# Scan of a hybrid layer: the doubling steps of two groups of token tiles are issued together over the four quarters of the array

## The chip, the cores and the metric

One core of one Trainium2 chip runs the program. The time is that of the device for one execution, in microseconds; the median of three runs is given. The records are of one further, profiled execution.

## What is computed

One layer of a backbone: a mixer of two branches (a 2-D Fourier transform, and a bidirectional RWKV-7 scan over 16 heads of 64 channels), normalised, then a feed-forward part with 16 experts. The change lies in the scan alone:

```python
def wkv7_scan(r, w, k, v, kk, a, s0, reverse):
    def step(S, inp):
        r_t, w_t, k_t, v_t, kk_t, a_t = inp
        sa = jnp.einsum('bhij,bhj->bhi', S, -kk_t)
        S = (S * w_t[:, :, None, :] + sa[..., None] * (kk_t * a_t)[:, :, None, :]
             + v_t[..., None] * k_t[:, :, None, :])
        y = jnp.einsum('bhij,bhj->bhi', S, r_t)
        return S, y
```

## The kernel before, in words

`scan_phase` computes the recurrence in blocks of 128 tokens: four of the latent sequence, one of the context. It walks over eight **tiles** of 128 channels, two heads each (`tiles`, `body`). In a tile, for each token block (`p`, in the order ORDER), direction and head, a unit triangular matrix of 128 x 128 has to be inverted; these are 5 x 4 problems. Each falls into two diagonal quarters of 64 x 64, which stand in partitions 0 to 63 and 64 to 127 and are inverted by doubling, and one quarter off the diagonal.

A tile has these stages:

1. *Pair products* (`pair_products`, L883 to L898): per token block the products of keys and queries, which DVE masks (L1192), and the quarters in both orientations, which ACT evicts to TT_diag and M (L772, L773; M is named `x` in the records, as it lies in spare room of that name). All four quarters of the PE array are used there: rows and columns 0 to 63 and 64 to 127 in every combination. POOL makes the start values: TT_diag (`tt_start`, L653 and L655), the masked blocks Mo of a level (`m_off`, L672) and T (`t_start`, L660, L664). Between the blocks stand pieces of the previous tile's norm.
2. *Doubling*, levels 1 to 5 (a round each, `rd` = 0 to 4), over three groups of token blocks: group 0 has two, group 1 two, group 2 one. In a round each group does Z = Mo by TT_diag (`z_step`, L914), ACT evicts Z (L781), then the increments of TT (L939) and of T (L945) in `t_step`, and DVE adds them (L1235, in the fifth round L1238 into TT; L1241). Group b's next Z needs its TT, its next TT increment needs its T. A group's matmuls alternate between two quarters of the array: rows 0 to 63 into output partitions 0 to 63, and rows 64 to 127 into 64 to 127. `m_off` overwrites the only buffer Mo, and so waits until the Z of the level before has been issued.
3. *Last level* (`rd` = 5): Z (L920), the product with T (L935), evicted by ACT into TT (L793).
4. *Chain* (L973 on): the states over the token blocks and the output.

Into the rounds are woven 14 **slots** that prepare the next tile, three per round, on every engine in the same order (`front`): slot 0 is a product of 512 columns (L830), its sigmoids on ACT (L701, after a table load) and a square (L706); slot 1 the same for 128 columns, after which DVE runs five prefix scans (L1092); then the norm of keys, the rates, exponentials (L739), operands (L1119 to L1124), all on DVE. Slot 0 on PE waits until ACT has read what stood in the bank before, slot 1 until slot 0's sigmoids are done. Two pieces of the previous tile's norm lie on DVE in slots 2 (L1179) and 14 (L1183, the gate product). The last tile has no slots; a few fillers (L951) keep PE going. The order on each engine is written out by hand, and an engine does its list strictly in order. A wait on PE holds everything behind it.

What sets the order around the change on PE in round 1 (lines 1026 on):

```python
                for rd in range(TOP):
                    z_step(i, NGR * rd)
                    z_step(i, NGR * rd + 1)
...
                    for b in range(NGR):
                        if b == 1:
                            z_step(i, NGR * rd + 2)
                        if not last and PER_ROUND * rd + b < NSLOT:
                            front(PER_ROUND * rd + b, i + 1, 1 - m)
...
                        t_step(i, NGR * rd + b)
```

## Time and profile before

| | us |
|---|---|
| median of 3 runs (2639.53 to 2642.63) | 2639.89 |
| the profiled execution | 2641.52 |
| its span, first to last instruction | 2639.6 |
| PE busy (matmuls) | 2402.4 (91%) |
| DVE busy | 1012.1 (38%) |
| ACT busy | 639.0 (24%) |
| POOL busy | 364.8 (14%) |
| L914 busy, L939 busy (3200 records each) | 116.6, 120.2 |

The span holds the projection, the scan (from 493 to about 1307 us), the merge and the experts. Busy time is the union of an engine's records. A matmul in f32 stands as two records in the profile, each as long as its passage through the array; records that overlap count once. The engine's idle time before an instruction stands in brackets with what released it; an idle engine costs something only where the end waits for it. PEclk is the share of TensorE's full clock that was granted. The shares of the whole span say little on the scan, since its stages have different limits; the windows below take its stages one by one.

### The profile page before, as it was taken

How to read it: one execution, taken by the hardware profiler on the slowest of the kernel's cores; microseconds unless marked ns; L12 is line 12 of the kernel's file. 1: busy time of each engine (PE TensorE's matmuls, PEld its weight loads, DVE VectorE, ACT ScalarE, POOL GpSimd, SP SyncE). 2: the span in 40 equal slices, each digit the busy share in tenths (PEclk: the TensorE clock that was granted, in tenths of full speed). 3: DMA queues.
4: the chain of work that ended last, by engine and by line, in shares of the span. 5: the costliest groups of instructions: out<-in, count | busy, mean ns of one | idle time of the engine just before them, and what ended most of it. 6: DMA issues, size and time to landing. Idle time of an engine off the chain costs nothing. (4 is left out here: it accounts for less than half of the span.)

```text
span 2639.6 us, 58406 instructions
## 1 busy us (share of the span) xinstructions
PE 2402.4 (91%) x26357; PEld 1534.5 (58%) x26357; DVE 1012.1 (38%) x1765; ACT 639.0 (24%) x1209; POOL 364.8 (14%) x405
## 2 busy tenths in 40 slices
PE   6999996689998999989799669999999999999993
PEld 4999995587787777778695423333333333333331
DVE  3343311658467576574345511212121212121214
ACT  2121222435445345343320101111111111111111
POOL 0000000315325225134003400000000000000000
PEclk7999998799999999999999779999999999999997
DMA  9362331010000000000191199999999999999974
GB/s 352 133 220 95 114 114 61 20 44 5 27 25 5 27 26 5 27 8 5 46 315 63 55 396 385 404 384 404 382 404 385 404 385 403 384 404 382 404 295 164
DMA packets 181119, 538.62 MB, mean 204 GB/s; under 512 B 13398, under 2 KB 54070, under 8 KB 180744
## 3 DMA queue, kind: packets, MB, share of 16 engines
q1 hardware_dynamic: 177704, 524.34, 52.3%
q0 software_dynamic: 3072, 10.49, 1.9%
q8 instruction: 209, 3.42, 0.5%
q14 instruction: 38, 0.31, 0.0%
q10 hardware_dynamic: 96, 0.05, 0.0%
HBM read 504.15 MB, written 30.70 MB: 203 GB/s over the span
## 5 line engine op out<-in xcount | busy, mean ns | idle before, releaser
L1815 PE MATMUL ps_h_lat<-w_piece,xT 128*64 128x512 f32 x2048 | 457.0, 599 | 10.9 <-DVE hidden L1937 7.5
L1815 PEld LDWEIGHTS ps_h_lat<-w_piece,xT 128*64 128x64 f32 x2048 | 145.9, 138 | 315.3 <-issue 315.3
L1840 PE MATMUL ps_y_lat<-w_piece,hiddenT 128*64 128x512 f32 x1024 | 232.6, 596 | 0.9 <-ACT hiddenT L1701 0.9
L1931 DVE TENSOR_TENSOR hidden<-sigmoid_lat,ps_h_lat 64x1024 f32<-64x1024 f32 x32 | 39.1, 1223 | 506.5 <-ACT sigmoid_ctx L1707 506.5
L1824 PE MATMUL ps_h_ctx<-w_piece,xT 128*16 128x512 f32 x2048 | 226.1, 593 | 0.0
L325 PE MATMUL ps_in<-hT_hi,w_in_hi 128*128 128x320 f32 x752 | 173.7, 312 | 2.7 <-issue 2.7
L672 POOL TENSOR_TENSOR Mo<-x,levels_sb 128x256 f32<-128x256 f32 x200 | 161.8, 832 | 99.0 <-PE ps_scan L914 98.9
L325 PE MATMUL ps_in<-hT_hi,w_in_lo 128*128 128x320 f32 x752 | 172.0, 310 | 0.0
L325 PE MATMUL ps_in<-hT_lo,w_in_hi 128*128 128x320 f32 x752 | 171.9, 310 | 0.0
L914 PE MATMUL ps_scan<-TT_diag,Mo 64*64 64x64 f32 x3200 | 116.6, 221 | 43.7 <-issue 26.9
L1840 PEld LDWEIGHTS ps_y_lat<-w_piece,hiddenT 128*64 128x64 f32 x1024 | 70.2, 137 | 138.3 <-issue 137.7
L1705 ACT ACTIVATE sigmoid_lat<-ps_h_lat 64x1024 f32<-64x1024 f32 x32 | 32.6, 1019 | 470.0 <-PE ps_h_lat L1815 470.0
L1824 PEld LDWEIGHTS ps_h_ctx<-w_piece,xT 128*16 128x16 f32 x2048 | 58.9, 97 | 139.9 <-issue 137.7
L914 PEld LDWEIGHTS ps_scan<-TT_diag,Mo 64*64 64x64 f32 x3200 | 106.3, 136 | 50.8 <-issue 49.3
L325 PEld LDWEIGHTS ps_in<-hT_hi,w_in_hi 128*128 128x128 f32 x752 | 126.2, 189 | 4.9 <-issue 4.7
L325 PEld LDWEIGHTS ps_in<-hT_lo,w_in_hi 128*128 128x128 f32 x752 | 126.5, 189 | 0.0
L325 PEld LDWEIGHTS ps_in<-hT_hi,w_in_lo 128*128 128x128 f32 x752 | 126.1, 189 | 0.0
L939 PE MATMUL ps_scan<-Z,T 64*64 64x64 f32 x3200 | 120.2, 222 | 5.6 <-ACT Z L781 5.3
L1756 POOL DMA_INDIRECT x_scratch<-ye,row_out x16 | 22.8, 1428 | 737.5 <-DVE ye L1944 737.5
L939 PEld LDWEIGHTS ps_scan<-Z,T 64*64 64x64 f32 x3200 | 107.2, 137 | 22.4 <-issue 19.0
L1192 DVE TENSOR_TENSOR NRR<-ps_scan,causal_sb 128x384 f32<-128x384 f32 x160 | 78.0, 549 | 104.7 <-PE ps_scan L884 104.6
L1849 PE MATMUL ps_y_ctx<-w_piece,hiddenT 128*16 128x256 f32 x2048 | 116.7, 380 | 0.0
(301 smaller groups left out, 3645.1 us busy)
## 6 DMA issues: line engine op xcount, KB each, us to landing
w_piece<-in_w_e SPq DMA_DIRECT2D x192, 2048.0 KB, 17.2
...
```

Of the source, the lines that this page charges most:

```text
L325: last = pe.matmul(wide[c % 2][:, b * 512:b * 512 + HALF], w, h[:, k, b * HALF:(b + 1) * HALF], start=(k == 0 and n == 0), stop=(k == KD - ...
L672: ins = g_.tensor_tensor(Mo[:, p, :, :].rearrange("p (e h) n -> p e h n", e=2), Mq[:, ORDER[p], 0:2, :, :], levels[:, l, :, :].unsqueeze(2 ...
L914: last = pe.matmul(ps_of(b_z(b), b)[hs, c, q, :], Mo[hs, p, q, :], TD[hs, p, q, :], start=True, stop=True)
L939: last = pe.matmul(ps_of(b_z(b), b)[hs, c, q, :], T[hs, p, q, :], Z[hs, p, q, :], start=True, stop=True)
L1192: v.tensor_tensor(NRR[:, p, :, :], src[:, 0:3 * P].rearrange("p (a n) -> p a n", a=3), causal[:, dr, :, :], ALU.mult).then_inc(s_am, 1)
L1705: act.activation(sg[UP, :], psA[UP, :], ACT.Sigmoid)
L1756: g_.indirect_dma_start(out=d["x1"], out_offset=bass.IndirectOffsetOnAxis(ap=row[j][:, 0:1], axis=0), in_=ye[j][:, :], in_offset=None, com ...
L1815: last = pe.matmul(psA[rows, cs], x[:, k, A], w[:, q, cs], start=(k == 0), stop=(k == KD - 1))
L1824: last = pe.matmul(psB[GRP[g], :], x[:, k, B], w[:, q, c * 512:(c + 1) * 512], start=(k == 0), stop=(k == KD - 1))
L1840: last = pe.matmul(psY[rows, :], hT[:, f, A], w[:, q, c * 512:(c + 1) * 512], start=(hf == 0 and f == 0), stop=(hf == 1 and f == FK - 1))
L1849: last = pe.matmul(psYB[GRP[g], 0:256], hT[:, f, B], w[:, q, g * 256:(g + 1) * 256], start=(hf == 0 and f == 0), stop=(hf == 1 and f == FK ...
L1931: v.tensor_tensor(hid[A, :], sg[UP, :], psA[UP, :], ALU.mult)
```

## The change

Token blocks 2 and 3 in the order (group 1) are CROSSED: their Z comes out in the other half of the partitions, and their T is held there too. So the matmuls of group 1 use the two quarters that group 0 leaves free, and `z_step` and `tt_step` take both groups together and alternate between them, four quarters in turn. The products that update T (`dt_step`) stay in two quarters each and stand by themselves; group 2's is issued after the next round's Z of both groups. For the crossed blocks the pair products compute T's start once more in the swapped place (8 matmuls a block), ACT evicts it (2 a block), and `t_start` masks it in place. Mo has two buffers, by the level's parity, and `m_off` waits for the Z of two levels before. The two pairs of fillers in the last level go. The orders on PE, ACT and DVE are written anew.

```diff
@@ -449,6 +449,7 @@
     NG, NPROB = NT, 4
     ORDER = [0, 3, 1, 2, 4]
     POS = {g: n for n, g in enumerate(ORDER)}
+    CROSSED = (2, 3)
     GROUPS, CHUNKS, BANKS = ((0, 2), (2, 4), (4, 5)), (slice(0, 4, 3), slice(1, 3, 1), slice(4, 5, 1)), ((0, 1), (2, 3), (4, 5))
     TOP = LEVELS - 1
     steps = [(b, l) for l in range(1, LEVELS) for b in range(len(GROUPS))]
@@ -495,7 +496,8 @@
 
         TT, M = [spare[:, n * NG * NPROB * P:(n + 1) * NG * NPROB * P].rearrange("p (g q n) -> p g q n", g=NG, q=NPROB)
                  for n in range(2)]
-        T, Z, Mo, TD = [sb(n, [P, NG, NPROB, HD]) for n in ("T", "Z", "Mo", "TT_diag")]
+        T, Z, TD = [sb(n, [P, NG, NPROB, HD]) for n in ("T", "Z", "TT_diag")]
+        Mo = [sb(f"Mo{n}", [P, NG, NPROB, HD]) for n in range(2)]
 
         y, gT = sb("y_T", [P, TOK])[:, :], sb("output_gate", [P, TOK])
         Mq = M.rearrange("p g q n -> p g (q n)")[:, :, 0:3 * 2 * HD].rearrange("p g (e h n) -> p g e h n", e=3, h=2)
@@ -657,7 +659,8 @@
                 def t_start(b):
 
                     for p in range(*GROUPS[b]):
-                        g_.tensor_tensor(T[:, p, :, :].rearrange("p (e h) n -> p e h n", e=2), Mq[:, ORDER[p], 0:2, :, :],
+                        low = T[:, p, :, :].rearrange("p (e h) n -> p e h n", e=2)
+                        g_.tensor_tensor(low, low if p in CROSSED else Mq[:, ORDER[p], 0:2, :, :],
                                          levels[:, 0, :, :].unsqueeze(2).broadcast_to([P, 2, 2, HD]), ALU.mult)
                     g_.drain()
                     flat = wide_of(T, b).rearrange("p c q n -> p (c q) n")
@@ -666,10 +669,10 @@
                 def m_off(n):
 
                     b, l = steps[n]
-                    if l > 1:
-                        g_.wait_ge(s_z, i * NS + n - NGR + 1)
+                    if l > 2:
+                        g_.wait_ge(s_z, i * NS + n - 2 * NGR + 1)
                     for p in range(*GROUPS[b]):
-                        ins = g_.tensor_tensor(Mo[:, p, :, :].rearrange("p (e h) n -> p e h n", e=2), Mq[:, ORDER[p], 0:2, :, :],
+                        ins = g_.tensor_tensor(Mo[l % 2][:, p, :, :].rearrange("p (e h) n -> p e h n", e=2), Mq[:, ORDER[p], 0:2, :, :],
                                                levels[:, l, :, :].unsqueeze(2).broadcast_to([P, 2, 2, HD]), ALU.mult)
                     ins.then_inc(s_mo, 1)
 
@@ -769,6 +772,8 @@
                 for n, g in enumerate(ORDER):
                     act.wait_ge(s_m, i * NG + n + 1)
                     for h in range(2):
+                        if n in CROSSED:
+                            act.activation(T[:, n, h::2, :], b_m(h)[:, 5 * HD:7 * HD].rearrange("p (e n) -> p e n", e=2), ACT.Copy)
                         act.activation(TD[:, n, h::2, :], b_m(h)[:, 3 * HD:5 * HD].rearrange("p (e n) -> p e n", e=2), ACT.Copy)
                         ins = act.activation(Mq[:, g, :, h, :], b_m(h)[:, 0:3 * HD].rearrange("p (e n) -> p e n", e=3), ACT.Copy)
                     ins.then_inc(s_ms, 1)
@@ -780,11 +785,9 @@
                         act.wait_ge(s_z, i * NS + NGR * rd + b + 1)
                         act.activation(wide_of(Z, b)[:, :, 0:nq, :], ps_of(b_z(b), b, nq), ACT.Copy).then_inc(s_zs, 1)
 
-                    evict(0)
-                    evict(1)
                     for b in range(NGR):
-                        if b == 1:
-                            evict(2)
+                        evict(b)
+                    for b in range(NGR):
                         if not last and PER_ROUND * rd + b < NSLOT:
                             front(PER_ROUND * rd + b, i + 1, 1 - m)
                         if rd == TOP - 1:
@@ -896,54 +899,60 @@
                     for x, xs in enumerate(HALVES):
                         for h, hs in enumerate(HALVES):
                             last = pe.matmul(b_m(h)[xs, (3 + dr) * HD:(4 + dr) * HD], B[dr][hs, at(x)], AR[m][dr][hs, g, 0, xs], start=True, stop=True)
+                    if n in CROSSED:
+                        for x, xs in enumerate(HALVES):
+                            for h, hs in enumerate(HALVES):
+                                last = pe.matmul(b_m(h)[HALVES[1 - x], (5 + dr) * HD:(6 + dr) * HD], AR[m][dr][hs, g, 0, xs], B[dr][hs, at(x)],
+                                                 start=True, stop=True)
                 last.then_inc(s_m, 1)
 
-            def z_step(i, n):
-                b, l = steps[n]
+            def problems(bs, l):
+
+                both = [[(b, c, p, q, x) for c, p in enumerate(range(*GROUPS[b])) for q in range(2 if l == TOP else NPROB) for x in range(2)]
+                        for b in bs]
+                return [one for pair in zip(*both) for one in pair]
+
+            def z_step(i, rd, bs):
+                l, n = rd + 1, NGR * rd + bs[-1]
                 if l < TOP:
                     pe.wait_ge(s_mo, i * ND + n + 1)
                 if l == 1:
-                    pe.wait_ge(s_tt0, i * NG + GROUPS[b][1])
+                    pe.wait_ge(s_tt0, i * NG + GROUPS[bs[-1]][1])
                 else:
                     pe.wait_ge(s_tt, i * ND + n - NGR + 1)
                 pe.sem_inc(s_pe_turn, 1)
...
+                for b, c, p, q, x in problems(bs, l):
                     if l < TOP:
-                        for q in range(NPROB):
-                            for hs in HALVES:
-                                last = pe.matmul(ps_of(b_z(b), b)[hs, c, q, :], Mo[hs, p, q, :], TD[hs, p, q, :], start=True, stop=True)
+                        last = pe.matmul(ps_of(b_z(b), b)[HALVES[x ^ (p in CROSSED)], c, q, :], Mo[l % 2][HALVES[x], p, q, :], TD[HALVES[x], p, q, :],
+                                         start=True, stop=True)
                     else:
-                        g = ORDER[p]
-                        for h in range(2):
-                            for dr, hs in enumerate(HALVES):
-                                os_ = HALVES[1 - dr]
-                                last = pe.matmul(ps_of(b_z(b), b, 2)[hs, c, h, :], Mq[os_, g, 2, h, :], TT[os_, g, 2 * dr + h, os_], start=True, stop=True)
-                last.then_inc(s_z, 1)
-
-            def t_step(i, n):
-                b, l = steps[n]
+                        g, os_ = ORDER[p], HALVES[1 - x]
+                        last = pe.matmul(ps_of(b_z(b), b, 2)[HALVES[x ^ (p in CROSSED)], c, q, :], Mq[os_, g, 2, q, :], TT[os_, g, 2 * x + q, os_],
+                                         start=True, stop=True)
+                last.then_inc(s_z, len(bs))
+
+            def tt_step(i, rd, bs):
+                l, n = rd + 1, NGR * rd + bs[-1]
                 pe.wait_ge(s_zs, i * NS + n + 1)
                 if l == 1:
-                    pe.wait_ge(s_ti, i * NGR + b + 1)
+                    pe.wait_ge(s_ti, i * NGR + bs[-1] + 1)
                 else:
                     pe.wait_ge(s_t, i * ND + n - NGR + 1)
                 pe.sem_inc(s_pe_turn, 1)
+                for b, c, p, q, x in problems(bs, l):
+                    hs, ts = HALVES[x], HALVES[x ^ (p in CROSSED)]
+                    if l == TOP:
+                        last = pe.matmul(ps_of(b_z(b), b, 2)[hs, c, q, :], T[ts, p, 2 * x + q, :], Z[ts, p, q, :], start=True, stop=True)
+                    else:
+                        last = pe.matmul(ps_of(b_z(b), b)[hs, c, q, :], T[ts, p, q, :], Z[ts, p, q, :], start=True, stop=True)
+                last.then_inc(s_dtt, len(bs))
+
+            def dt_step(b):
                 for c, p in enumerate(range(*GROUPS[b])):
-                    if l == TOP:
-                        for h in range(2):
-                            for dr, hs in enumerate(HALVES):
-                                last = pe.matmul(ps_of(b_z(b), b, 2)[hs, c, h, :], T[hs, p, 2 * dr + h, :], Z[hs, p, h, :], start=True, stop=True)
-                    else:
-                        for q in range(NPROB):
-                            for hs in HALVES:
-                                last = pe.matmul(ps_of(b_z(b), b)[hs, c, q, :], T[hs, p, q, :], Z[hs, p, q, :], start=True, stop=True)
-                last.then_inc(s_dtt, 1)
-                if l < TOP:
-                    for c, p in enumerate(range(*GROUPS[b])):
-                        for q in range(NPROB):
-                            for hs in HALVES:
-                                last = pe.matmul(ps_of(b_dt(b), b)[hs, c, q, :], Z[hs, p, q, :], T[hs, p, q, :], start=True, stop=True)
-                    last.then_inc(s_dt, 1)
+                    for q in range(NPROB):
+                        for hs in HALVES:
+                            last = pe.matmul(ps_of(b_dt(b), b)[hs, c, q, :], Z[hs, p, q, :], T[hs, p, q, :], start=True, stop=True)
+                last.then_inc(s_dt, 1)
 
             def fill(n):
 
@@ -1012,19 +1021,30 @@
                 pe.wait_ge(s_ms, i * NG + NG)
                 if not first:
                     pe.wait_ge(s_gs, i)
+                def slot(n):
+                    if not last and n < NSLOT:
+                        front(n, i + 1, 1 - m)
+
                 for rd in range(TOP):
-                    z_step(i, NGR * rd)
-                    z_step(i, NGR * rd + 1)
+                    z_step(i, rd, (0, 1))
+                    if rd:
+                        dt_step(2)
+                    z_step(i, rd, (2,))
                     if rd == TOP - 1:
                         turn(J_KT0, i, m, last)
-                    for b in range(NGR):
-                        if b == 1:
-                            z_step(i, NGR * rd + 2)
-                        if not last and PER_ROUND * rd + b < NSLOT:
-                            front(PER_ROUND * rd + b, i + 1, 1 - m)
-                        if rd == TOP - 1 and b:
-                            fill(2)
-                        t_step(i, NGR * rd + b)
+                        slot(PER_ROUND * rd)
+                        tt_step(i, rd, (0, 1))
+                        slot(PER_ROUND * rd + 1)
+                        tt_step(i, rd, (2,))
+                        slot(PER_ROUND * rd + 2)
+                    else:
+                        slot(PER_ROUND * rd)
+                        tt_step(i, rd, (0, 1))
+                        dt_step(0)
+                        slot(PER_ROUND * rd + 1)
+                        dt_step(1)
+                        tt_step(i, rd, (2,))
+                        slot(PER_ROUND * rd + 2)
                 fill(3)
                 pe.wait_ge(s_full, i * NGR + NGR)
                 part(i, m, CT, "X")
@@ -1222,23 +1242,38 @@
                         norm(n, i - 1, 1 - m)
                 for dr in range(2):
                     scaled_state(m, dr, 0)
+                def slot(n):
+                    if not first and n in (2, NSLOT):
+                        norm(N_BONUS if n == 2 else N_GATE, i - 1, 1 - m)
+                    if not last and n < NSLOT:
+                        front(n, i + 1, 1 - m)
+
+                def add_tt(rd, b):
+                    v.wait_ge(s_dtt, i * NS + NGR * rd + b + 1)
+                    if rd < TOP - 2:
+                        v.tensor_tensor(wide_of(TD, b), wide_of(TD, b), ps_of(b_z(b), b), ALU.add).then_inc(s_tt, 1)
+                    else:
+                        for hs in HALVES:
+                            ins = v.tensor_tensor(TT[hs, CHUNKS[b], :, hs], wide_of(TD, b)[hs], ps_of(b_z(b), b)[hs], ALU.add)
+                        ins.then_inc(s_tt, 1)
+
+                def add_t(rd, b):
+                    v.wait_ge(s_dt, i * ND + NGR * rd + b + 1)
+                    v.tensor_tensor(wide_of(T, b), wide_of(T, b), ps_of(b_dt(b), b), ALU.add).then_inc(s_t, 1)
+
                 for rd in range(TOP):
...
+                    if rd:
+                        add_t(rd - 1, 2)
+                    slot(PER_ROUND * rd)
+                    if rd < TOP - 1:
+                        add_tt(rd, 0)
+                        add_tt(rd, 1)
+                        add_t(rd, 0)
+                    slot(PER_ROUND * rd + 1)
+                    if rd < TOP - 1:
+                        add_t(rd, 1)
+                        add_tt(rd, 2)
+                    slot(PER_ROUND * rd + 2)
                 for n in CHAIN[:-1]:
                     state(i, m, n)
 
```

On **PE**, the first round of a middle tile; L914 is Z in the kernel before, L926 in the changed one, L939 or L947 TT's increment, L945 or L954 T's, L830 or L833 slots 0 and 1. Before:

```order
L914 MATMUL ps_scan<-TT_diag,Mo 64x64 x32
L830 MATMUL ps_scan<-lora,w_dec 128x512 x2
L939 MATMUL ps_scan<-Z,T 64x64 x16
L945 MATMUL ps_scan<-T,Z 64x64 x16
L914 MATMUL ps_scan<-TT_diag,Mo 64x64 x8
L830 MATMUL ps_scan<-lora,w_dec 128x128 x2
L939 MATMUL ps_scan<-Z,T 64x64 x16
L945 MATMUL ps_scan<-T,Z 64x64 x16
```

Changed:

```order
L926 MATMUL ps_scan<-TT_diag,Mo 64x64 x40
L833 MATMUL ps_scan<-lora,w_dec 128x512 x2
L947 MATMUL ps_scan<-Z,T 64x64 x32
L954 MATMUL ps_scan<-T,Z 64x64 x16
L833 MATMUL ps_scan<-lora,w_dec 128x128 x2
L954 MATMUL ps_scan<-T,Z 64x64 x16
L947 MATMUL ps_scan<-Z,T 64x64 x8
```

The 40 are Z of groups 0 and 1 (32) and of group 2 (8): group 2's Z now stands ahead of slot 0 and of the first TT increment.

On **DVE**, the same round from slot 0's end on; L1235 or L1254 is the add of TT, L1241 or L1262 that of T, L1092 or L1112 the prefix scans of slot 1. Before:

```order
L1235 TENSOR_TENSOR TT_diag<-TT_diag,ps_scan 128x512
L1241 TENSOR_TENSOR T<-T,ps_scan 128x512
L1092 SCALAR_TENSOR_TENSOR G_T<-one_sb,sg 128x128 x5
L1094 TENSOR_SCALAR half_total<-G_T 128x5
L1235 TENSOR_TENSOR TT_diag<-TT_diag,ps_scan 128x512
L1241 TENSOR_TENSOR T<-T,ps_scan 128x512
```

Changed:

```order
L1254 TENSOR_TENSOR TT_diag<-TT_diag,ps_scan 128x512 x2
L1262 TENSOR_TENSOR T<-T,ps_scan 128x512
L1112 SCALAR_TENSOR_TENSOR G_T<-one_sb,sg 128x128 x5
L1114 TENSOR_SCALAR half_total<-G_T 128x5
L1262 TENSOR_TENSOR T<-T,ps_scan 128x512
L1254 TENSOR_TENSOR TT_diag<-TT_diag,ps_scan 128x256
```

Both pair groups' adds of TT now stand ahead of the prefix scans.

## Rows read from the trace of the kernel before

**Rows 1.** Windows of the fourth tile: rounds 1, 2 and 5 (us, busy per engine).

```profile
core 0: us, PE busy (x) PEld busy (x) DVE busy (x) ACT busy (x) POOL busy (x), PEclk, DMA share, GB/s
815.08:826.67 11.59, 10.52 (x252) 8.67 (x254) 8.38 (x14) 7.44 (x12) 10.12 (x15) 1.00 0.01 3
826.67:837.42 10.75, 10.04 (x260) 8.58 (x257) 9.88 (x15) 7.51 (x12) 4.44 (x5) 1.00 0.01 4
...
855.32:865.93 10.61, 8.67 (x238) 7.79 (x240) 10.25 (x16) 2.20 (x4) 0.00 (x0) 1.00 0.01 3
```

**Rows 2.** Timeline of PE, fourth tile: start, us, engine, line, operation, idle before.

```profile
800.35 0.41 PE L898 MATMUL ps_scan<-AR,B 64*64 64x64 f32 x16
...
815.08 2.08 PE L914 MATMUL ps_scan<-TT_diag,Mo 64*64 64x64 f32 x64 [1.08 <-ACT x L773]
...
820.91 0.68 PE L914 MATMUL ps_scan<-TT_diag,Mo 64*64 64x64 f32 x16 [0.68 <-POOL Mo L672]
```

**Rows 3.** Timeline of POOL, fourth tile.

```profile
812.69 0.92 POOL L653 TENSOR_TENSOR TT_diag<-TT_diag,level_sb 128x256 f32<-128x256 f32 x1 [0.29 <-ACT x L773]
...
814.43 1.30 POOL L672 TENSOR_TENSOR Mo<-x,levels_sb 128x256 f32<-128x256 f32 x2
...
820.09 0.67 POOL L672 TENSOR_TENSOR Mo<-x,levels_sb 128x256 f32<-128x256 f32 x1
```

**Rows 4.** Timeline of ACT, fourth tile.

```profile
812.10 0.29 ACT L772 ACTIVATE TT_diag<-ps_scan 128x128 f32<-128x128 f32 x1
...
819.37 1.28 ACT L701 ACT_TABLE_LOAD   x1 [1.57 <-DVE par_cur L1133]
820.66 1.26 ACT L701 ACTIVATE sg<-ps_scan,par_cur 128x512 f32<-128x512 f32 x2
822.04 0.83 ACT L706 ACTIVATE e_T<-rkv_T,par_cur 128x640 f32<-128x640 f32 x1
...
823.04 0.62 ACT L701 ACTIVATE sg<-ps_scan,par_cur 128x128 f32<-128x128 f32 x2
...
840.02 1.06 ACT L781 ACTIVATE Z<-ps_scan 128x512 f32<-128x512 f32 x2
```

**Rows 5.** Timeline of DVE, fourth tile, from the prefix scan to the last adds.

```profile
823.73 2.82 DVE L1092 TENSOR_TENSOR_SCAN G_T<-one_sb,sg 128x128 f32<-128x128 f32 x5 [2.75 <-ACTq L703]
...
827.22 0.69 DVE L1235 TENSOR_TENSOR TT_diag<-TT_diag,ps_scan 128x512 f32<-128x512 f32 x1 [0.43 <-issue]
827.82 0.68 DVE L1241 TENSOR_TENSOR T<-T,ps_scan 128x512 f32<-128x512 f32 x1
...
839.52 1.07 DVE L1119 TENSOR_TENSOR AR<-rkv_T,e_T 128x640 f32<-128x640 f32 x1 [0.53 <-ACT e_T L739]
840.52 1.29 DVE L1121 SCALAR_TENSOR_TENSOR AR<-kk_T,e_T 128x640 f32<-128x640 f32 x1
...
845.27 1.68 DVE L1092 TENSOR_TENSOR_SCAN G_T<-one_sb,sg 128x128 f32<-128x128 f32 x5
...
856.47 0.82 DVE L1121 SCALAR_TENSOR_TENSOR AR<-kk_T,e_T 128x640 f32<-128x640 f32 x1
...
866.73 0.83 DVE L1183 TENSOR_TENSOR y_T<-y_T,output_gate 128x640 f32<-128x640 f32 x1
867.47 0.84 DVE L1238 TENSOR_TENSOR x<-TT_diag,ps_scan 64x256 f32<-64x256 f32 x2
868.35 0.42 DVE L1241 TENSOR_TENSOR T<-T,ps_scan 128x256 f32<-128x256 f32 x1
```

**Rows 6.** The last tile: a window after PE's wait in round 1, then PE's timeline.

```profile
1231.94:1235.36 3.42, 3.42 (x72) 3.42 (x68) 1.06 (x2) 0.25 (x1) 3.30 (x6) 0.50 0.02 5
...
1230.76 0.95 PE L914 MATMUL ps_scan<-TT_diag,Mo 64*64 64x64 f32 x15 [1.82 <-POOL Mo L672]
...
1235.96 2.03 PE L914 MATMUL ps_scan<-TT_diag,Mo 64*64 64x64 f32 x63
...
1257.62 2.03 PE L914 MATMUL ps_scan<-TT_diag,Mo 64*64 64x64 f32 x64
...
1269.91 1.55 PE L973 MATMUL ps_scan<-Vt,NRR 128*128 128x64 f32 x12
```

17 lines of the change are left out of this document (removed).

## The prediction

> **What bounds the kernel now.** I read the windows of one steady tile of the scan first (the fourth of eight), then the timelines of its engines, then the last tile, which prepares no successor. The windows say that in the doubling stretch the PE is not alone: DVE is busy 9.88 of 10.75 us in round 2 and 10.25 of 10.61 in round 5 [rows 1]. Between the adds of the doubling stand the jobs that prepare the next tile, and DVE does them in a fixed order. Only in round 1 has it room (8.38 of 11.59): there it waits 2.75 us for a sigmoid before the first prefix scan, L1092 at 823.73 [rows 5]. After that I find it idle for 0.43 us (at 827.22) and 0.53 (at 839.52) and hardly more until the last TT add at 867.47. So the end of a steady tile is set by **when that prefix scan starts**, and by the 43.74 us of DVE work from there to 867.47. PE time saved after 823.73 is worth little; PE time lost before it is worth all of itself.
>
> In the last tile there are no such jobs. Its rounds take (1257.62 - 1235.96) / 3 = 7.22 us [rows 6], and PE sets them.
>
> **The rate in four quarters.** A matmul shows as two records, and one record lasts 0.22 us from issue to end. L945 and L914 use two quarters: 64 records in 2.08 us [rows 2] are (2.08 - 0.22) / 31 = 0.060 us for each further pair. L898 in the pair products already uses all four: 16 records in 0.41 us are (0.41 - 0.22) / 3 = 0.063 for each further four [rows 2]. I take twice the rate, so a step of both pair groups, 64 records, falls from 1.87 to 0.93 us. The bound below is no gain at all. Per round the PE saves 0.93 on Z and 0.93 on TT; T's product stays in two quarters. Against that rate speaks the order: the quarters of L898 alternate between the two halves of the rows at each matmul, the new Z step goes lower, lower, upper, upper. No row of before shows that order, so it is a rival below. The Trainium skill, TensorE: Matmul & The Clock Gate, Part 3 (what overlaps and what doesn't), says that a weight load overlaps running matmuls only when the row group differs; by that rule half of the loads of a Z step would stand exposed and the pairing would give nothing.
>
> **The pair products.** For groups 2 and 3 in the order, 8 matmuls each are added in four quarters: 4 fours of 0.06 = 0.23 us of PE, twice, so 0.47. ACT gets two evictions each of the size of L772, which lasts 0.29 [rows 4]; with the overlap of neighbours I take 0.17, so 0.34 per group. They lie on the path: POOL's L653 at 812.69 waited for just that eviction [rows 3]. POOL's chain from there moves by 0.47 + 0.34 = **+0.81 us**; POOL's own work is unchanged.
>
> **Round 1.** This is where I expect the loss.
> - Z of both pair groups needs the masked blocks of the second, which end at 814.43 + 1.30 [rows 3]; now 816.54. Z01 goes from 816.6 to 817.5, not from 815.08.
> - PE's next instruction is now Z of group 2, ahead of the front's product and of TT. Its masked block is the end of POOL's chain, 820.09 + 0.67 [rows 3]; before, PE went there only after slot 0 and the first group's products and still waited 0.68 [rows 2]. Now the block comes at 821.57 and PE goes on at 821.7. It stands from 817.5 to 821.7, some **4.2 us, with everything behind it**: slot 0, TT01, and all that waits for those.
> - Slot 0 of the front begins at 822.2 and its product is there by 823.3. ACT evicts Z of group 2 first, loads its table from 822.8 (1.28), does the two sigmoids (1.26) to 825.4; before, the table load began at 819.37 [rows 4]. PE's slot 1 is done by 825.95. ACT does the square (0.83), then slot 1's sigmoids at 826.25 (before 823.04), 0.62, and the prefix scan starts at 826.95 instead of 823.73: **+3.2 us**. TT01, T0 and T1 fit beside this and cost nothing; if ACT were faster, T0 and T1 would be late next.
>
> **From the scan to the end of the tile.** Of the 43.74 us, one TT add (0.60 from start to start, 827.22 to 827.82 [rows 5]) is now done before the scan, and the gate product (866.73 to 867.47, 0.74) moves behind the last TT add. The waits of 0.43 and 0.53 have cover now, one new wait for an exponential, some 0.6, appears in round 3, as ACT must evict all of Z first. That is 42.04, so the last TT add starts at 869.0 (+1.5). But the last T add now stands behind the gate product: 0.88 + 0.74 + 0.15 of drain later, 870.8 against 868.35 [rows 5], **+2.4 us**. The last level hangs on both adds as before: Z2 waits for the last TT, then come slot work (0.7), TT01, and six evictions in a row on ACT; that sum ends +2.3 to +2.4. The fillers that go there lay beside it.
> The second buffer of masked blocks lets POOL run a level ahead. Where POOL is busy DVE's SBUF operations are slower: five scan pieces take 2.82 us there [rows 5]. One level less of such company I put at -0.4. Steady tile: **+2.0**.
>
> **Clock.** In the last tile PE stood 1.82 us (L914 at 1230.76) and then ran 3.42 us at half clock, granted 0.50 [rows 6]. The new stand of 4.2 us is longer and in every tile. Half clock for 3.42 us loses at most 1.71; what follows the stand on the path is Z2 (0.47) and slot 0 (some 1.1), the rest ACT's. Bounds 0 and 1.7; I take +0.6, as the half-clock stretch may begin before the stand ends.
>
> **Last tile.** Z2 at 1230.76 + 0.81; then 0.47 + 0.93 + 0.93 + 0.93 + 0.47 = 3.73 and 1.7 of half clock: round 2 starts at 1237.0 (before 1235.96). A round then is Z01 0.93, 1.47 to evict both (1.06 for two evictions [rows 4], at 840.02, and some 0.2 at either end; Z2 and the third group's T product, 0.94, lie inside), TT01 0.93, T0 0.93, T1 0.93, TT2 0.47: 5.66. Three rounds to 1254.0. Round 5 and the last level hang on DVE's adds of half height, about 11.5: 1265.5 against 1269.91 [rows 6], **-4.4**.
>
> **Sum.** Seven tiles at 2.0 + 0.6, that is +18.2; the first tile has no gate product and longer waits to recover, which I count as -0.8; the last -4.4. +13.0 on the profiled execution's 2641.5, so 2654.5; the median of the runs shown is 1.6 below it, hence **2653**. (Seven are the first seven; what lies outside the scan is not touched.) PE saves some 10 us of busy time per tile, 80 in all, and the kernel gains none of it, since DVE has none to give.
>
> **The rivals.**
> - *The stand is longer in effect*: half clock also falls on rounds 3 to 6, where PE now waits for DVE about 2 us in each. One such stretch on the path per tile: 7 x 1.7 = +12, 2665. For it: the granted clock fell already in the last tile for one wait. Against: in rounds 3 to 5 PE has slack.
> - *Four quarters don't run together* in the new order of rows. Z01 and TT01 stay at 1.87: in round 1 slot 1 of the front comes some 0.6 later behind T0, and 0.5 more at the last level, +1 in each of seven tiles, and the last tile's rounds are 7.5 instead of 5.7, +7: 2667. For it: that order has no row; against it: L898 with another order runs in fours.
> - *The loss is taken back*: slots and adds on DVE end earlier than my sum, the 3.2 us shrinks below 1, and the last tile's gain pays for the rest: 2640, no difference.
> - *Faster*: DVE's contention with POOL is what sets the rounds. The scan takes 2.82 us beside POOL and 1.68 without, L1121 1.29 and 0.82 [rows 5]; with six such operations per tile that is 1.14 + 6 x 0.43, about 3.7 us. If running ahead takes POOL out of DVE's way altogether, a tile goes from +2.6 to about -0.7: 2653 - 7 x 3.3 = 2630. It decides from 1.9 us per tile on. Against it: POOL does the same work, and in the same first rounds in which DVE's long operations stand. A variant with PE as the bound throughout, 8 x 10 us, would give 2560; rows 1 speak against it.
>
> **Numbers.** A measurement of this kernel tells 0.2%, 5.3 us, from no change. The forecast's mechanism with its bounds (2645 to 2660) 0.50; the longer half clock 0.10; the quarters 0.10; taken back 0.15; faster 0.15. So slower 0.70, same 0.15, faster 0.15. The range goes from 2632, which takes in the recovery and the edge of the gain, to 2669, the two dearer rivals.
>
> **What would show it.** Right: PE's wait before the second L926 group of round 1, released by POOL, some 4 us in each tile; the first prefix scan 3 us later against the start of the tile's pair products; tiles 2.6 us longer from one first L883 to the next; rounds 2 to 4 of the last tile at 5.7; four records of Z01 per 0.06 us; the granted clock at 0.50 after round 1. Wrong: prefix scan not later, or DVE's 42 us from scan to last TT add much shorter, say 38: then POOL's company was the bound. If Z01 takes 2 us, the quarters didn't overlap.

## The result, and the profile after

| | before | after |
|---|---|---|
| median of the runs (us) | 2639.7 (2639.2 to 2642.6, 4 runs) | 2705.0 (2689.1 to 2713.4, 4 runs) |
| profiled execution, and its span | 2641.5, 2639.6 | 2713.4, 2711.6 |
| mean granted clock of that run | 0.960 | 0.927 |

The change makes the kernel slower by 2.4% (ratio 1.0240, 95% interval 1.0221 to 1.0258), 65 us. The prediction said slower, 2653, with 2669 as the upper end: the direction was right, the size was not. The profiled execution is the slowest of the four, so the stage lengths below add up to 72 us and not to 65.

I cut a steady tile at five starts that both traces have: the tile's first pair product, the first Z of round 1, the first prefix scan, the last TT add, the chain's first product. The windows between them, the fourth tile of before:

```profile
core 0: us, PE busy (x) PEld busy (x) DVE busy (x) ACT busy (x) POOL busy (x), PEclk, DMA share, GB/s
798.38:815.09 16.71, 15.63 (x294) 12.73 (x294) 11.49 (x23) 9.77 (x26) 10.19 (x15) 1.00 0.04 11
815.09:823.73 8.64, 7.57 (x196) 6.38 (x198) 5.51 (x9) 5.36 (x9) 8.21 (x13) 1.00 0.02 4
823.73:867.47 43.74, 38.57 (x1077) 34.80 (x1074) 41.30 (x65) 20.53 (x37) 15.53 (x18) 1.00 0.01 3
867.47:871.42 3.95, 3.82 (x59) 2.25 (x57) 1.25 (x4) 2.40 (x9) 0.00 (x0) 1.00 0.43 128
871.42:901.25 29.83, 27.28 (x254) 24.31 (x254) 7.43 (x28) 9.09 (x26) 0.00 (x0) 1.00 0.11 35
```

The same windows of after, its third tile:

```profile
714.58:733.12 18.54, 16.09 (x324) 13.18 (x325) 13.08 (x25) 10.45 (x30) 11.21 (x16) 1.00 0.04 10
733.12:745.36 12.24, 9.33 (x210) 7.36 (x212) 4.22 (x7) 5.47 (x9) 11.74 (x18) 0.58 0.01 3
745.36:786.24 40.88, 30.35 (x1059) 26.34 (x1055) 37.57 (x64) 20.03 (x37) 9.83 (x10) 1.00 0.01 3
786.24:791.73 5.49, 3.74 (x57) 2.52 (x57) 2.07 (x5) 2.36 (x8) 0.00 (x0) 0.68 0.29 90
791.73:827.16 35.43, 33.14 (x254) 30.14 (x254) 7.43 (x28) 9.08 (x26) 0.00 (x0) 0.81 0.10 30
```

The column to read is PEclk. Before, every stage of this tile has the granted clock at 1.00 (2.4 GHz). After, the stages behind the first Z and behind the last TT add do not: the clock is at 0.50 (1.2 GHz) for 10.2 us from 733.6 and for 17.1 us from 788.2, and so in each later tile up to the seventh. The chain (last window) has the same 254 records, and takes 35.4 us instead of 29.8. Tiles 2 to 7 last 112.6 to 112.8 us each; before, they last 102.3 to 102.9, 102.5 on the mean. Seven tile lengths give +69.8, the last tile and what follows it +2.6, the start -0.4: the 72.0 us between the spans.

PE in round 1 of after, to be laid beside [rows 2] (a **stand** is a wait of PE with work queued behind it):

```profile
733.12 1.64 PE L926 MATMUL ps_scan<-TT_diag,Mo 64*64 64x64 f32 x64 [2.45 <-POOL Mo L675]
737.67 1.12 PE L926 MATMUL ps_scan<-TT_diag,Mo 64*64 64x64 f32 x16 [2.91 <-POOL Mo L675]
738.72 2.08 PE L833 MATMUL ps_scan<-lora,w_dec 64*128 64x512 f32 x4
740.73 1.98 PE L947 MATMUL ps_scan<-Z,T 64*64 64x64 f32 x64
742.49 1.72 PE L954 MATMUL ps_scan<-T,Z 64*64 64x64 f32 x32
744.13 0.49 PE L833 MATMUL ps_scan<-lora,w_dec 64*128 64x128 f32 x4
744.56 1.15 PE L954 MATMUL ps_scan<-T,Z 64*64 64x64 f32 x32
...
747.38 1.16 PE L926 MATMUL ps_scan<-TT_diag,Mo 64*64 64x64 f32 x64
```

Both stands are there, each ended by POOL's masked blocks: 2.45 us ahead of the pair groups' Z, 2.91 ahead of the third group's. Between 733.6 and 743.8 everything is slow: the pair Z 1.64 where the same 64 records take 1.16 at 747.38, the front's product 2.08, a T product 1.72 where the next takes 1.15. DVE and ACT show what hangs on it, against [rows 4, 5]:

```profile
742.78 1.28 DVE L1254 TENSOR_TENSOR TT_diag<-TT_diag,ps_scan 128x512 f32<-128x512 f32 x2 [7.34 <-PE ps_scan L947]
...
745.36 1.69 DVE L1112 TENSOR_TENSOR_SCAN G_T<-one_sb,sg 128x128 f32<-128x128 f32 x5 [0.43 <-ACTq L706]
```

```profile
738.83 0.38 ACT L786 ACTIVATE Z<-ps_scan 128x256 f32<-128x256 f32 x1 [2.94 <-PE ps_scan L926]
739.23 1.28 ACT L704 ACT_TABLE_LOAD   x1
...
744.67 0.62 ACT L704 ACTIVATE sg<-ps_scan,par_cur 128x128 f32<-128x128 f32 x2 [1.62 <-PE ps_scan L833]
```

ACT evicts the third Z before it can load its table (739.23), then waits 1.62 us for slot 1, whose product stands behind PE's slow T product. The scan starts 30.78 us after the tile's start; before, 25.35.

The second place is the last level. PE, after:

```profile
784.71 0.64 PE L954 MATMUL ps_scan<-T,Z 64*64 64x64 f32 x16
787.23 0.45 PE L930 MATMUL ps_scan<-x 64*64 64x64 f32 x8 [1.88 <-DVE x L1257]
787.61 0.80 PE L849 MATMUL ps_scan<-ident_sb,K 128*128 128x128 f32 x5
788.34 1.55 PE L945 MATMUL ps_scan<-Z,T 64*64 64x64 f32 x40
789.83 1.14 PE L960 MATMUL ps_scan<-causal_sb 128*128 128x384 bf16 x3
791.73 2.82 PE L982 MATMUL ps_scan<-Vt,NRR 128*128 128x64 f32 x12 [0.76 <-ACT x L796]
```

The third group's Z is again ahead of everything. It waits 1.88 us for DVE's last TT add, with the front's transposes and the pair groups' product behind it; what that product needs last, DVE's add of T, was done at 786.32. One us after the stand the clock falls, and the chain's first twelve records take 2.82 us instead of 1.55 [rows 6].

### The profile page after: what moved, and what is told of

Same layout as the page of the kernel before. It is cut to its first block and busy times, and to the rows that moved or that the text cites. A ratio compares the mean times of both kernels' runs of the same rounds, so it can differ in the third digit from the quotient of the medians.

```text
span 2711.6 us, 58790 instructions
## 1 busy us (share of the span) xinstructions
PE 2390.9 (88%) x26581; PEld 1517.4 (56%) x26581; DVE 994.5 (37%) x1765; ACT 640.9 (24%) x1241; POOL 353.1 (13%) x405
## 5 line engine op out<-in xcount | busy, mean ns | idle before, releaser
L675 POOL TENSOR_TENSOR Mo<-x,levels_sb 128x256 f32<-128x256 f32 x200 | 153.7, 798 | 54.0 <-PE ps_scan L926 54.0
L926 PE MATMUL ps_scan<-TT_diag,Mo 64*64 64x64 f32 x3200 | 82.7, 233 | 83.0 <-POOL Mo L675 44.2
L954 PE MATMUL ps_scan<-T,Z 64*64 64x64 f32 x3200 | 118.9, 224 | 5.7 <-issue 5.7
L926 PEld LDWEIGHTS ps_scan<-TT_diag,Mo 64*64 64x64 f32 x3200 | 72.3, 144 | 90.9 <-issue 89.7
L954 PEld LDWEIGHTS ps_scan<-T,Z 64*64 64x64 f32 x3200 | 108.7, 140 | 8.7 <-issue 6.1
```

Source lines behind the costliest of these rows:

```text
L675: ins = g_.tensor_tensor(Mo[l % 2][:, p, :, :].rearrange("p (e h) n -> p e h n", e=2), Mq[:, ORDER[p], 0:2, :, :], levels[:, l, :, :].unsq ...
L926: last = pe.matmul(ps_of(b_z(b), b)[HALVES[x ^ (p in CROSSED)], c, q, :], Mo[l % 2][HALVES[x], p, q, :], TD[HALVES[x], p, q, :], start=Tru ...
L954: last = pe.matmul(ps_of(b_dt(b), b)[hs, c, q, :], Z[hs, p, q, :], T[hs, p, q, :], start=True, stop=True)
```

## The experiments

Three theories were open. **O**: the place of the third group's Z, a stand in round 1, is the loss. **C**: the loss is TensorE's clock, at the chain above all. A third says that pairing itself leaves PE so idle that the clock falls whatever the order. Each was timed beside runs of the kernel before on the same chip (medians of 2639 to 2641), and the ratios are to those; differences from after (2705) are between medians of separate timings. A fill product is one of `fill(n)`, a bf16 product of 128x384 that nothing waits for; three take 0.66 us at full clock. First the stage lengths of tiles 2 to 7 in all kernels, cut as above from one profiled execution of each (us):

| kernel | median | to Z | to scan | to last TT | to chain | to next tile | tile |
|---|---|---|---|---|---|---|---|
| before | 2639.7 | 16.7 | 8.6 | 43.1-43.8 | 3.9 | 29.8 | 102.3-102.9 |
| after | 2705.0 | 18.5 | 12.2-12.3 | 40.9-41.0 | 5.5 | 35.4-35.5 | 112.6-112.8 |
| e1_order | 2669.8 | 18.5 | 6.8-7.4 | 42.5-43.3 | 5.0-5.7 | 29.8-35.5 | 104.0-109.4 |
| e4_before_z2ahead | 2667.6 | 16.7 | 12.3 | 43.2-43.4 | 3.9 | 29.8 | 106.0-106.2 |
| e6_r1fill | 2684.0 | 19.2 | 9.1 | 41.6-42.4 | 5.0-6.2 | 29.8-33.9 | 104.7-110.7 |
| e7_tailfill | 2665.3 | 18.5 | 11.5-11.8 | 40.9 | 5.0 | 29.8 | 105.8-106.0 |
| e8_bothfill | 2676.1 | 18.5 | 9.8 | 41.6-42.4 | 5.0-5.2 | 29.8-34.0 | 105.5-109.0 |
| e9_order_tail | 2658.0 | 18.5 | 6.8-8.7 | 42.1-43.0 | 5.0 | 29.8-33.9 | 102.5-108.3 |
| e11_lateall | 2626.9 | 18.5 | 6.8-7.4 | 41.8-42.6 | 3.4-4.5 | 29.8 | 100.4-101.7 |
| e12_pairprod | 2644.3 | 17.2 | 8.1 | 43.5-44.8 | 3.9-4.1 | 29.8 | 102.6-104.0 |
| e13_onebuffer | 2630.5 | 18.5 | 6.8-8.7 | 42.0-43.0 | 3.4-4.5 | 29.8 | 100.9-102.8 |
| e14_before_twobuf | 2641.1 | 16.7 | 8.7 | 43.6-44.5 | 3.9 | 29.8 | 102.7-103.6 |
| e15_best | 2630.1 | 18.5 | 6.8 | 42.3-42.7 | 3.3-4.5 | 29.8 | 100.7-102.3 |
| e16_before_nofill | 2637.7 | 16.7 | 8.6 | 43.7-44.0 | 3.3-3.6 | 29.8 | 102.3-102.7 |

**The order alone, in the changed kernel**

```diff
-                    z_step(i, rd, (2,))
+                    if rd: z_step(i, rd, (2,))
...
                         dt_step(0)
+                        if rd == 0: z_step(i, rd, (2,))
```

(and ScalarE's third eviction of round 1 behind its first slot)

> The changed kernel, but in round 1 alone the Z step of the third group is issued behind slot 0, TT of the pair groups and T of the first, as it stood before the change, and ScalarE evicts it after the front's first slot. Theory O (the place of that step is the loss: a stand of 2.91 us in each tile with slot 0 and TT behind it): the first prefix scan comes 2.5 to 3.5 us earlier, 7 x 3 = 21 us, about 2684. Theory C (the loss is TensorE's clock: 10.2 us at half clock in round 1 and 17.1 us at the chain): the clock falls already behind the first stand (2.45 us, before the pair groups' Z), which stays; only what TensorE did not wait for is gained, and the chain stays at half clock: 2690 to 2700. Both together (the order cures half of round 1, the chain's share stays): 2680. If nothing is gained (2700 or more), the stand cost nothing and was cover for other work.

Measured: 2669.8 (ratio 1.0119, 1.0090 to 1.0147), 35 us less than after, more than any of the three said. The scan comes 6.8 or 7.4 us behind Z, 5 us earlier. The 2.45 us stand stays, and yet the half clock between Z and the scan is 3.4 us long in tiles 2, 3, 5 and 6, and absent in 4 and 7, where it was 10.2. At the chain the clock is low in five of seven tiles; here is the fourth, with the stretch from the scan to the last TT add at 0.84 on the mean as well:

```profile
837.22:880.54 43.32, 34.65 (x1044) 30.78 (x1042) 40.48 (x64) 19.70 (x35) 15.83 (x19) 0.84 0.01 3
...
885.56:919.41 33.85, 31.56 (x253) 28.47 (x254) 7.43 (x28) 9.08 (x26) 0.00 (x0) 0.85 0.11 32
```

So order and clock are not apart here: another order in round 1 alone changed the clock in several later places too.

**The stand alone, in the kernel before**

```diff
                     z_step(i, NGR * rd + 1)
+                    if rd == 0:
+                        z_step(i, NGR * rd + 2)
```

(the later place is skipped in round 1, ScalarE's eviction moved likewise)

> The kernel before, with the third group's Z step of round 1 moved ahead of slot 0 and of the first TT on TensorE, and its eviction likewise; nothing in four quarters, one buffer of masked blocks. It measures the stand by itself. The prediction's step: the stand is some 3.5 us, the prefix scan 2.5 to 3.2 us later, 7 x 2.5 = 18 us, 2658, with half clock for one stretch of 3.4 us. Theory O says the same or more (2660 to 2670). Theory C says that the clock falls for longer than before the change only if TensorE's other gaps are as in the changed kernel; here the rounds still have their old products, so 2650 to 2660 and no half clock at the chain. If it gives 2700, the order alone is the whole loss.

Measured: 2667.6 (1.0105, 1.0088 to 1.0121), +27 us. PE in round 1, then the window to the scan:

```profile
828.02 2.08 PE L916 MATMUL ps_scan<-TT_diag,Mo 64*64 64x64 f32 x64 [1.10 <-ACT x L773]
833.83 0.68 PE L916 MATMUL ps_scan<-TT_diag,Mo 64*64 64x64 f32 x16 [3.73 <-POOL Mo L672]
834.44 1.80 PE L832 MATMUL ps_scan<-lora,w_dec 64*128 64x512 f32 x4
```

```profile
828.02:840.31 12.29, 8.56 (x179) 6.77 (x181) 5.51 (x9) 5.58 (x9) 9.86 (x15) 0.86 0.01 3
```

The stand of 3.73 us delays the scan by 3.6 us, and costs 3.5 us of the tile. With it come 3.4 us at half clock per tile, not 10.2, and none at the chain. A stand of this length does not by itself make the long stretches. The time lies in the range that O gave (2660 to 2670); that the chain keeps its clock is what C said, whose range (2650 to 2660) was too low.

**Fill products in the stands of round 1**

```diff
+                    if rd == 0: fill(12)
                     z_step(i, rd, (0, 1))
                     if rd: dt_step(2)
+                    else: fill(14)
                     z_step(i, rd, (2,))
```

> The changed kernel with fill products in round 1 alone: 12 of 128x384 (some 0.164 us each, 2.0 us) ahead of the pair groups' Z, 14 (2.3 us) between it and the third group's Z; they lie in the two stands of 2.45 and 2.91 us and nothing waits for them. Theory C: round 1 is at full clock, its path of front product (2.08 to 1.35), TT (1.98 to 1.16) and T (1.72 to 1.15) is 2 to 2.6 us shorter in each tile, 8 x 2.3 = 18 us, 2686; the chain's half clock stays. Theory O (the wait, not the clock): nothing, 2700 to 2705. If the fills stand in the way, slower than 2705.

Measured: 2684.0 (1.0176, 1.0159 to 1.0192), 21 us less. Nothing was moved and PE was given more to do, and the kernel is faster. The 12 fills were a little long: Z starts 0.65 us later. The number is C's, the place is not: C left the chain at half clock, and the chain takes 29.8 to 33.9 us here instead of 35.4. Over tiles 2 to 7, which are 23.7 us shorter together, the way to the scan gives 15.2 us, the stretch from the scan to the chain takes 7.2 back, and the chain gives 15.8, though no fill stands there.

**Fill products in the stand of the last level**

```diff
                         dt_step(2)
+                    if rd == TOP - 1:
+                        pe.wait_ge(s_t, i * ND + NGR * (TOP - 2) + 1)
+                        fill(11)
                     z_step(i, rd, (2,))
```

> The changed kernel with 11 fill products (1.8 us) in the last level, between the pair groups' Z and the third group's Z, where TensorE stands 1.88 us for a TT add. Theory C: no half clock from the last level through the chain (17.1 us in each tile); from last TT add to the next tile's first product as before the change, 35.5 to 30 and 5.5 to 4.5 us, so 5 to 6.5 us in each of eight tiles, 40 to 52 us: 2653 to 2665. Theory O: nothing from this, 2700 to 2705. A third reading, that the clock falls for the sparse rounds before it and not for this one wait: half clock stays, and the time within 5 us of 2705.

Measured: 2665.3 (1.0091, 1.0075 to 1.0108), 40 us less, for 88 added products, at the upper edge of C's range. The last level and the chain of its third tile:

```profile
774.00:779.02 5.02, 3.59 (x63) 2.26 (x60) 2.08 (x5) 2.36 (x8) 0.00 (x0) 1.00 0.31 97
779.02:808.85 29.83, 27.28 (x253) 24.30 (x254) 7.43 (x28) 9.11 (x26) 0.00 (x0) 1.00 0.12 36
```

The chain is back at 29.83 us, in all tiles. This is the largest single share of the loss: 112.6 to 105.9 us per tile, 6.7 us, of which 5.6 are the chain's, 0.5 lie between the last TT add and the chain, and 0.6 in round 1, whose half clock is 6.8 us long from the third tile on instead of 10.2. O said nothing would come of it, and falls as the whole answer.

**Both fills**: 8 and 14 products in round 1, 11 in the last level.

> The changed kernel with the fill products of both earlier runs (8 and 14 in round 1, 11 in the last level): every stand stays where it is, TensorE's clock alone is cured. Theory C in sum: 20 us from round 1 and 40 from the chain, each measured alone, should add up: a tile of 18.5 + 9.5 + 41.7 + 5.0 + 29.8 = 104.5 us against 102.5 before the change, 2645 to 2655, which is where the prediction stood (2653). If the two don't add (the clock falls elsewhere instead), 2660 or more. If below 2642, the stand of the third group's Z costs nothing once the clock is full.

Measured: 2676.1 (1.0131, 1.0116 to 1.0147): the gains don't add, and it is dearer than with the fills of the last level alone. The chains of tiles 2 to 4 are like the first line, those of 5 to 7 like the second, the first tile's lies between (32.8):

```profile
780.30:810.13 29.83, 27.28 (x254) 24.31 (x254) 7.43 (x28) 9.10 (x26) 0.00 (x0) 1.00 0.12 36
...
990.77:1024.81 34.04, 31.76 (x254) 28.66 (x254) 7.43 (x28) 9.09 (x26) 0.00 (x0) 0.85 0.10 32
```

Here PE is filled in all three stands, and the clock fell at those chains all the same. The tiles do differ ahead of them: in round 3 PE stands 2.91 us in one piece in tiles 5 to 7, and 0.75 and 1.37 us in tiles 2 to 4. No run takes that stand out by itself, and with the order alone a tile with such a stand (3.19 us, the third) keeps its chain at full clock; so the cause stays open. Tiles 2 to 4, with full clock in round 1 and at the chain and 3.4 to 6.8 us of half clock between, are worth having: 105.5 us, of which 28.3 to the scan and 42.3 from there to the last TT add. That is about the changed kernel with its stands and without the loss of clock: **+3.0 us per tile**.

One thing more differs. The five prefix scans, in the third tile with the last fills alone and in that with both:

```profile
733.12 2.08 DVE L1115 TENSOR_TENSOR_SCAN G_T<-one_sb,sg 128x128 f32<-128x128 f32 x5
```

```profile
732.97 3.40 DVE L1119 TENSOR_TENSOR_SCAN G_T<-one_sb,sg 128x128 f32<-128x128 f32 x5 [0.42 <-ACTq L706]
```

Against the tile's start the second comes 1.9 us earlier, and so lies beside GpSimd's masked blocks for 90% of its time, the first for 30%. Of those 1.9 us it gives 1.3 back.

**Order and last fills together**

> The third group's Z of round 1 behind slot 0, TT and T of the first (as in the earlier run of the order), with the 11 fill products of the last level. Theory: the loss has two parts, the stand in round 1 and the half clock at the chain; with both away a tile is 18.5 + 7.0 + 42.8 + 5.0 + 29.8 = 103.2 us, 0.7 above before, the last tile some 3 us shorter: 2638 to 2647. If the half clock only moves to other rounds and costs there, 2650 to 2660. If the pairing itself loses more than the pair products' 1.8 us, above 2660.

Measured: 2658.0 (1.0063, 1.0048 to 1.0079), 11 above the theory's range and inside the one for a half clock that moves elsewhere. Its best tile is 102.5, as before the change; in three of seven the chain ran below full clock (33.9). PE has other stands there, 3.19 us in round 3 and 1.44 just ahead of the chain; the latter is in the run with the last fills alone too, where no chain falls.

**The pairing with the old order throughout**

```diff
                     z_step(i, rd, (0, 1))
                     if rd: dt_step(2)
-                    z_step(i, rd, (2,))
...
                         tt_step(i, rd, (0, 1))
                         dt_step(0)
+                        z_step(i, rd, (2,))
```

(on PE in all rounds and in the last level, there without `dt_step` and with one `fill(2)` behind it; ScalarE evicts the third Z behind its first slot in all rounds)

> The changed kernel with the old places of the third group's Z in every round and in the last level, on TensorE and on ScalarE: only the pairing in four quarters, its pair products and the second buffer of masked blocks are left of the change. No fill products beside the two of the kernel before. Theory (the order of Z is the cause, the half clock its consequence): no stand over 2 us but that before round 1, the step from the last TT add to the chain back from 5.0-5.5 to 4 us, full clock at the chain: 2630 to 2642. Rival (pairing leaves TensorE idle enough to lose the clock by itself, whatever the order): half clock at the chain in most tiles, 29.8 to 33-35 us, 2660 to 2680.

Measured: **2626.9** (2624.1 to 2631.3; ratio to before 0.9957, 0.9944 to 0.9971): 78 us less than after, and 12.7 less than before. Its third tile:

```profile
692.08:710.62 18.54, 16.09 (x324) 13.18 (x325) 13.08 (x25) 10.45 (x30) 11.22 (x16) 1.00 0.04 10
710.62:718.04 7.42, 7.41 (x211) 5.61 (x212) 4.13 (x7) 5.44 (x9) 6.99 (x11) 0.77 0.01 2
718.04:759.88 41.84, 32.34 (x1064) 28.25 (x1060) 40.37 (x63) 20.27 (x37) 14.93 (x18) 0.96 0.02 4
759.88:763.30 3.42, 2.70 (x54) 1.59 (x54) 2.08 (x5) 2.25 (x8) 0.00 (x0) 1.00 0.22 82
763.30:793.13 29.83, 27.28 (x254) 24.31 (x254) 7.43 (x28) 9.11 (x26) 0.00 (x0) 1.00 0.15 43
```

The chain is at 1.00 in every tile. The third theory falls for the chain: PE is busy for 85.8 us of this tile, less than the 92.7 of after and the 92.9 of before, and keeps its clock there. Some half clock stays where DVE covers PE: one or two stretches of 3.4 us in most tiles, where the kernel before has none in tiles 3 to 7. The step from the last TT add to the chain is 3.42, shorter than before the change. DVE is busy 40.37 of 41.84 us from the scan on, so it bounds what is left. The one `fill(2)` was not taken out by itself.

**The pair products alone, in the kernel before**: in `pair_products` the eight crossed products of two blocks, and their evictions into T, which GpSimd then overwrites.

> The kernel before with only the added pair products of the two crossed groups and their ScalarE evictions into T (GpSimd overwrites them afterwards, as its own start of T is left as it was). Prediction's step: GpSimd's chain +0.81 us in each tile, the scan with it: 7 x 0.8 = 5.7 us, 2647. From the changed kernel's profile, where the pair groups' Z begins 1.83 us later instead of the 1.55 forecast: 2645 to 2650. Hidden after all: within 2 us of 2641. Dearer than costed (over 1.2 us per tile): 2650 or more.

Measured: 2644.3 (1.0019, 1.0010 to 1.0028), +4.6. GpSimd's chain moved as costed:

```profile
815.89 0.67 POOL L653 TENSOR_TENSOR TT_diag<-TT_diag,level_sb 128x256 f32<-128x256 f32 x1 [1.11 <-ACT x L775]
```

That is 15.13 us behind the tile's start (800.76); in [rows 3] it is 14.31 (812.69 - 798.38): +0.82. But the scan comes no later (25.3 us behind the tile's start, as before). The 0.6 us per tile lie behind its start, and most of them in the scans themselves, which have GpSimd beside them for more of their time (80% instead of 70%) and take 3.24 us instead of 2.82 [rows 5]:

```profile
826.05 3.24 DVE L1099 TENSOR_TENSOR_SCAN G_T<-one_sb,sg 128x128 f32<-128x128 f32 x5 [2.02 <-ACTq L703]
```

**One buffer of masked blocks**, in the version of 2626.9 (its edit is shown), and **two buffers**, in the kernel before (the edit the other way):

```diff
-                    if l > 2: g_.wait_ge(s_z, i * NS + n - 2 * NGR + 1)
+                    if l > 1: g_.wait_ge(s_z, i * NS + n - NGR + 1)
-   Mo[l % 2][...]
+   Mo[0][...]
```

> The version with the old places of the third group's Z (2626.9), but with one buffer of masked blocks and GpSimd's old wait. Prediction's step: running a level ahead takes some of GpSimd's company from VectorE, 0.4 us per tile: +3, 2630. If the buffer is what made that version gain (the Z of a round is ready for TensorE earlier), 2634 to 2642. If the second buffer is worth nothing, within 2 us of 2627.

> The kernel before with the second buffer of masked blocks alone. If pairing in four quarters brings nothing and the buffer is the whole gain: 2625 to 2632. By the prediction's 0.4 us of less company per tile: 2637. If the rounds of the kernel before wait for nothing that the buffer gives: within 2 us of 2640. Slower than 2643 would mean that GpSimd now lies beside VectorE's longest operations.

Measured: 2630.5 (0.9963, 0.9949 to 0.9977) and 2641.1 (1.0010, 1.0001 to 1.0019). The buffer alone brings nothing; in the reordered version the medians are 3.5 us apart, with intervals that overlap. In the kernel before it makes the scans dearer, as GpSimd, which does not stop for Z there any more, works beside all of them:

```profile
824.27 3.68 DVE L1093 TENSOR_TENSOR_SCAN G_T<-one_sb,sg 128x128 f32<-128x128 f32 x5 [2.77 <-ACTq L704]
```

That is 0.86 us more than in [rows 5], and one of DVE's 128x640 products behind them is cheaper (0.98 us on the mean instead of 1.21): the company moves, it does not go. So the gain of 12.7 us over before is mostly not the buffer's. It is not shown to be the pairing's either: the version keeps DVE's new order as well, with a TT add ahead of the scan and the gate product behind the last one, and has one `fill(2)` less. In the traces a tile is 1.5 us shorter on the mean, of which 1.3 lie between the scan and the last TT add, where DVE bounds; the last tile, which PE bounds, reaches its chain 1.5 us sooner. No run has DVE's order without the pairing.

**More fills and the gate product behind the last T add**

```diff
+                    if rd == 0: fill(8)
                     z_step(i, rd, (0, 1))
...
+                    if rd == 2: pe.wait_ge(s_t, ...); fill(8)
```

> The version with the old places of Z (2626.9), with VectorE's gate product behind the last T add, 8 fill products ahead of the first Z step and 8 in the third round behind T of the third group, where TensorE stands 2.45 and 2.64 us. Theory: the scan comes after 6.8 us in every tile (7.4 in some), 0.4 on the mean, and the last T add 0.85 us earlier, of which 0 to 0.4 reach the chain, as ScalarE's evictions set it: 3 to 6 us in all, 2621 to 2624. If these places are not on the path, 2625 to 2628. If the fills come in the way of TT in round 3, above 2630.

Measured: 2630.1 (0.9966, 0.9954 to 0.9978): no gain. The scan is at 6.8 us in every tile, where it was at 6.9 on the mean, and the time from there to the last TT add is 0.4 longer (42.4 against 42.0 on the mean). Taking away most of the half clock that was left brought nothing here.

**The kernel before without its fills in the last level**

> The kernel before without the two pairs of fill products in its last level, which the change also took out. If their absence (not the stand of 1.88 us before the third group's Z) is what halves the clock at the chain: 17.1 us of half clock in each tile there and some 5.7 us more per tile, 2675 to 2690. If the stand is the cause: full clock at the chain, 2636 to 2642. In between (a few tiles fall): 2645 to 2660.

Measured: 2637.7 (0.9993, 0.9984 to 1.0002). The change also dropped these fills, and by themselves they are not what keeps the clock: without them the chain is at full clock in every tile. They did lie on the path: the step from the last TT add to the chain is 3.3 us in most tiles instead of 3.9.

## Why the prediction was right or wrong

*DVE bounds from the prefix scan on: right.* In after it is busy 37.6 of 40.9 us there, in the version of 2626.9 40.4 of 41.8.

*The rate in four quarters: right.* 64 records of the pair Z take 1.16 us from first issue to last end, and (1.16 - 0.22) / 15 = 0.063 per four, as in [rows 2] for the other order of quarters. That rival is out. By the rule of the Trainium skill, TensorE: Matmul & The Clock Gate, Part 3, that a weight load overlaps running matmuls only when the row group differs, half of the loads should have stood exposed here; the trace disagrees, and the trace decides.

*Pair products, round 1, scan to last TT: right where round 1 has its full clock.* Forecast: scan at 28.57 us behind the tile's start (826.95 - 798.38), 42.04 from there to the last TT add. Tiles 2 to 4 of the run with both fills have 28.3 and 42.3. GpSimd's +0.81 was +0.82. In after the stand ahead of the third group's Z is 2.91 us and not 4.2: the pair groups' Z starts 0.3 us later than forecast and takes 1.64 us instead of 0.93, partly at half clock. The stand of 2.45 us ahead of the pair groups' Z follows from its later start, but the clock term did not look at it.

*Behind the last TT add:* forecast some +0.9 more; at full clock 5.02 against 3.95, +1.1. Tile in all +2.0 forecast, +3.0 measured in those tiles. Of the 1.0 us between, 0.4 is the term for GpSimd's company (below), and 0.4 that the sum starts from the fourth tile of before, which is that much over the mean.

*The clock term, +0.6 per tile with bounds 0 and 1.7: this step failed.* It is 112.6 - 105.5 = 7.1 us per tile in the profiled executions, twelve times the term and four times its upper bound, and seven of them are 50 of the 72 us between those two. Two mistakes are in it. I took the length of the half-clock stretch, 3.42 us, from the one wait that the trace of before had, as if it were a property of a stand; it was 10.2 and 17.1. And I looked for the cost behind the stand I was pricing, in round 1. There the slow clock delays the scan by 2.5 us (30.8 behind the tile's start, against 28.3), and 1.4 of them come back: the later scan falls into a gap of GpSimd's and takes 1.69 us instead of 3.40. The chain costs 5.6 us, and the step ahead of it 0.5. They lie behind a stand in the last level that my sum had as a line of ScalarE's evictions ("Z2 waits for the last TT, then come slot work") without a price for PE's 1.88 us. The chain is the stage in which nothing covers PE: at half clock it grows by 5.6 us on 29.8.

*The rival "half clock also falls on rounds 3 to 6"* was nearest in its mechanism, with a wrong place and price: one stretch of 1.7 per tile, 2665.

*Last tile: -4.4 forecast, nothing gained.* Its first stages up to the chain take 62.55 us against 61.68. Rounds 2 to 4 take 6.90 on the mean (from 1305.70 to 1326.39) instead of 7.22, and not 5.66:

```profile
1312.50:1319.30 6.80, 5.69 (x249) 5.48 (x248) 2.89 (x6) 1.36 (x3) 3.18 (x5) 1.00 0.02 5
```

```profile
1316.29 0.86 PE L947 MATMUL ps_scan<-Z,T 64*64 64x64 f32 x43 [0.76 <-issue]
```

0.76 us of the difference is a stand in the middle of the pair groups' TT step, released by nothing that the trace shows. Round 5 and the last level, forecast 0.8 us shorter, are 1.5 longer (13.8 us from 1326.39 against 12.3). And the last chain loses to the clock as well. It is at 0.50 from 1341.2 to 1351.4:

```profile
1340.21 1.98 PE L982 MATMUL ps_scan<-Vt,NRR 128*128 128x64 f32 x12 [0.78 <-ACT x L796]
```

Its product L1009 starts 23.91 us behind this row; before, the same product (L1000) starts 19.60 us behind the chain's start. Of these 4.3 us 1.7 are left at the end of the program; where the others are made up was not followed.

*GpSimd's company, -0.4: not got.* In after the five scans take 1.69 us instead of 2.82, but only because they start late: at 745.36 GpSimd's run of masked blocks has just ended (738.97 + 6.32). Where the scan is on time in a kernel with two buffers, GpSimd is beside it for 90% of it or more, and it takes 3.4 to 3.7 us. With the buffer as the only change in the kernel before the tile is not shorter (102.7 us or more, against 102.3 to 102.9). Running a level ahead put the company onto the scans; the rival *faster* rested on its going away. (That rival takes 0.43 us for each of six operations; the row that it names has 1.29 - 0.82 = 0.47, which makes 4.0 us and not 3.7.)
